# FoX values made token by token for four heads at once, the residual kept in DRAM during the heads, and gate tiles ahead of the scores

## The reference

```python
def fox_shared_kv(h, kv_norm_g, w_kv, b_forget):
    proj = rmsnorm(h, kv_norm_g) @ w_kv              # (528, 2048 + 2048 + 16)
    k, v, f_logit = jnp.split(proj, [D_INNER, 2 * D_INNER], axis=-1)
    ...                                              # 16 heads of 128 columns
    cum = jnp.cumsum(log_sigmoid(f_logit + b_forget), axis=1)

def fox_layer(h, norm_g, w_in, w_out, k, v, cum):
    q, r = jnp.split(rmsnorm(h, norm_g) @ w_in, 2, axis=-1)
    q = q.reshape(...) * FOX_HEAD_DIM ** -0.5
    for start, end in zip(bounds[:-1], bounds[1:]):  # causal blocks of 128 queries
        s = q[start:end] @ k[:end].T + cum[start:end, None] - cum[None, :end]
        p = softmax(where(causal, s, NEG_INF))
        outs.append(p @ v[:end])
    return h + (o * silu(r)) @ w_out
h = rmsnorm(h, final_norm_g); return h[:, N_META:]
```

## Time and profile before

| | us |
|---|---|
| median of 3 runs | 1025.69 (1025.11 to 1025.74) |
| time of the profiled execution | 1027.1 |
| span in its profile | 1025.3 |
| PE busy | 1013.7 (99%) |
| PEld busy | 950.4 (93%) |
| DVE busy | 638.4 (62%) |
| ACT busy | 521.8 (51%) |
| granted PE clock, mean | 0.996 |

### The profile page before, as it was taken

The page is one execution under the profiler, slowest core; times in us unless marked ns, Lnnn a source line. Parts: engine busy times, 40 slices in busy tenths (PEclk is TensorE's granted clock), DMA queues, the critical chain, the costliest instruction groups (busy, mean ns, idle before and its releaser), DMA issues.

```text
span 1025.3 us, 18641 instructions
## 1 busy us (share of the span) xinstructions
PE 1013.7 (99%) x7655; PEld 950.4 (93%) x7655; DVE 638.4 (62%) x1100; ACT 521.8 (51%) x932; POOL 34.3 (3%) x69
## 2 busy tenths in 40 slices
PE   8999999999999999999999999999999999999997
PEld 7999999999999999998999999999999999988886
DVE  6875666577567784447665656655656566576433
ACT  6754644654474553336554545454545555564321
POOL 0000000000000000000101000000000000010000
PEclk9999999999999999999999999999999999999998
DMA  8221221221122122222444333332434332331312
GB/s 286 70 77 63 83 84 49 76 83 64 62 87 79 63 70 96 91 96 65 135 110 89 110 89 86 94 102 89 110 97 102 104 94 77 99 87 67 119 42 82
DMA packets 34838, 92.98 MB, mean 91 GB/s; under 512 B 3888, under 2 KB 12976, under 8 KB 34752
## 3 DMA queue, kind: packets, MB, share of 16 engines
q1 hardware_dynamic: 34320, 91.62, 29.3%
q10 hardware_dynamic: 432, 0.15, 0.1%
HBM read 89.43 MB, written 2.13 MB: 89 GB/s over the span
## 4 chain that ended last, share of the span: by engine, by line
PE 98%; DMA 1%; DVE 0%; ACT 0%; issue 0%; DVEq 0%; SPq 0%; ACTq 0%
PE psum L1385 81%; PE psum L1701 3%; PE psum L1510 2%; PE psum L1684 2%; PE psum L1438 1%; PE psum L1458 1%; PE psum L1672 1%; PE psum L1671 1%; PE psum L1673 1%; PE psum L1506 1%; PE psum L1479 1%; DMA hT<-xT 1%; PE psum L1689 1%; PE psum L1504 0%; PE psum L1436 0%; PE psum L1408 0%
## 5 line engine op out<-in xcount | busy, mean ns | idle before, releaser
L820 DVE TENSOR_TENSOR w_lo<-raw,w_hi 128x1024 fp32r<-128x1024 f32 x143 | 173.5, 1223 | 28.4 <-ACT w_hi L431 28.3
L431 ACT ACTIVATE w_hi<-raw 128x1024 fp32r<-128x1024 f32 x143 | 149.6, 1052 | 34.8 <-PE psum L1385 34.1
L1385 PE MATMUL psum<-xh,w_hi 128*128 128x264 f32 x768 | 159.1, 288 | 2.7 <-DVE xl L842 1.5
L1385 PE MATMUL psum<-xl,w_hi 128*128 128x264 f32 x768 | 155.9, 285 | 0.0
L1385 PE MATMUL psum<-xh,w_lo 128*128 128x264 f32 x768 | 155.3, 283 | 0.0
L1385 PEld LDWEIGHTS psum<-xh,w_hi 128*128 128x128 f32 x768 | 118.5, 189 | 4.2 <-issue 2.3
L1385 PEld LDWEIGHTS psum<-xl,w_hi 128*128 128x128 f32 x768 | 119.5, 188 | 0.0
L1385 PEld LDWEIGHTS psum<-xh,w_lo 128*128 128x128 f32 x768 | 119.1, 189 | 0.0
L1385 PE MATMUL psum<-zh,w_hi 128*128 128x264 f32 x512 | 106.0, 288 | 0.0
L1385 PE MATMUL psum<-y_lo,w_hi 128*128 128x264 f32 (+2 forms) x400 | 104.8, 314 | 0.0
L1385 PE MATMUL psum<-zl,w_hi 128*128 128x264 f32 x512 | 104.0, 285 | 0.0
(11 more groups left out here) (266 smaller groups left out, 1851.3 us busy)
## 6 DMA issues: line engine op xcount, KB each, us to landing
raw<-w_all SPq DMA_DIRECT2D x143, 512.0 KB, 3.3
sub<-sums SPq DMA_DIRECT2D x16, 264.0 KB, 7.1
sub<-sums SPq DMA_DIRECT2D x16, 200.0 KB, 6.5
sub<-sums SPq DMA_DIRECT2D x16, 136.0 KB, 4.7
hT<-xT SPq DMA_DIRECT2D x8, 264.0 KB, 6.7
outT<-hT SPq DMA_DIRECT2D x8, 256.0 KB, 2.5
sub<-sums SPq DMA_DIRECT2D x16, 72.0 KB, 3.5
raw<-w_all SPq DMA_DIRECT2D x2, 256.0 KB, 5.1
```

The costliest lines, as they stand in the source:

```text
L431: nc.scalar.activation(w_hi[:, n % HI_RING, :], raw[:, n % LO_RING, :], ACT.Copy).then_inc(hi_made, 1)
L820: nc.vector.tensor_tensor(w_lo[:, n % LO_RING, :], raw[:, n % LO_RING, :], w_hi[:, n % HI_RING, :].bitcast(F32), ALU.subtract).then_inc(lo ...
L1385: i = nc.tensor.matmul(o, w[a][:, k % KT, :], x[b][:, k, c0:c1], start=k == first and a == b == 0, stop=k == last and a == 1)
```

## The change

- **Values by token.** The value strips, their copy and the transposes go. For four heads at once (a group) the normed activations `zh`, `zl` are stationary, a block of 128 tokens at a time, and the weights of the four heads move, 512 columns (`fox_values`). Banks 4 to 7 take the four blocks. ACT and DVE write `fv_hi`, `fv_lo` from there for all four heads, in the order of blocks 3, 2, 0, 1. Each chunk now holds two contraction tiles by 512 columns, four chunks to a group.
- **End tokens.** Their values come from a product in plain f32 of its own (`end_values`, job m): `z_end`, 16 tokens, is stationary, and the raw weights move, in four column groups of the array. ACT and DVE add up the four partial sums. The splits of a group's first chunks on DVE wait for it, since `w_lo` is written over `raw`.
- **Order.** Group 0 stands before the first head; a group g stands after head 4g-1. Before the scores of a head stand the first two contraction tiles of its gate strip r, three after a group; in the kernel before none (one in the last head).
- **Residual.** `fv_hi` and `fv_lo` now lie where `hT` lies. The 512 tokens of `hT` are stored to DRAM during the first layer's output product and loaded back after the last head's attention.

```diff
 def fox_step(h):
-    jobs = [f"r{h}"] + more[:1] + more[1:] + [f"a{h}"] + ([f"x{h + 1}"] if more else [])
-    return jobs + ([f"v{h + 2}"] if h + 2 < FOX_HEADS else [])
+    group = (h + 1) // VH if more and (h + 1) % VH == 0 else None
+    return ([f"r{h}"] + more[:1] + ([] if group is None else [f"m{group}"]) + more[1:] + [f"a{h}"]
+            + ([] if group is None else [f"u{group}"]))
...
-        + ["k0", "LOWF", "q0", "v0", "x0", "v1"] + [j for h in range(FOX_HEADS) for j in fox_step(h)] + [f"w{d}" for d in range(KT)])
+        + ["k0", "LOWF", "m0", "q0", "u0"] + [j for h in range(FOX_HEADS) for j in fox_step(h)] + [f"w{d}" for d in range(KT)])
...
+    elif _job[0] == "u":
+        PLACE[_job] = 8
...
+            keep = {CHUNK[f"W{d + 1}b"] + LO_RING: d for d in range(1, KT - 1)}
+            keep.update({CHUNK["W1b"] + LO_RING: 0, CHUNK["k0"] + LO_RING: KT - 1})
...
+                if n in keep:
+                    d = keep[n]
+                    sp.wait_ge(h_made, d + 1)
+                    sp.dma_start(h_keep[:, d, :], hT[:, d, META:T]).then_inc(h_kept, 16)
+                if n == CHUNK["w1b"] + LO_RING:
+                    done(sp, f"a{FOX_HEADS - 1}")
+                    for d in range(KT):
+                        sp.dma_start(hT[:, d, META:T], h_keep[:, d, :]).then_inc(h_back[d], 16)
...
+            def fox_values_hi(g):
+                done(act, f"u{g}")
...
+                for b in U_ORDER:
+                    nc.scalar.activation(fv_hi[:, b, :], bank(4 + b), ACT.Copy, scale=rtok[:, b:b + 1]).then_inc(fvhi_made, 1)
...
+            def fox_values_lo(g):
+                for n, b in enumerate(U_ORDER):
+                    dve.wait_ge(fvhi_made, NBLK * g + n + 1)
+                    nc.vector.scalar_tensor_tensor(fv_lo[:, b, :], bank(4 + b), rtok[:, b:b + 1], fv_hi[:, b, :].bitcast(F32),
+                                                   op0=ALU.mult, op1=ALU.subtract).then_inc(fvlo_made, 1)
...
+            def end_values(g):
...
+                for k in range(KT):
+                    r = 32 * (k % 4)
+                    w = raw[:, CHUNK[f"u{g}{k // 2}"] % LO_RING, :].rearrange("p (k n) -> p k n", k=2)
+                    i = nc.tensor.matmul(bank(slot(job), 0, VH * P, r, r + META), z_end[:, k, :], w[:, k % 2, :], start=k < 4, stop=k >= 4)
+                i.then_inc(job_done, 1)
...
+            def fox_values(g):
+                if g:
+                    pe.wait_ge(alo_made, 4 * VH * g)
...
+                    for k in (2 * part, 2 * part + 1):
+                        for b in range(NBLK):
+                            if g and k == 0 and b == NBLK - 1:
+                                pe.wait_ge(fy_made, VH * g)
+                            for a, p in ((0, 0), (0, 1), (1, 0)):
+                                i = nc.tensor.matmul(bank(4 + b), xk[a][:, k, b * BLK:(b + 1) * BLK], w[p][:, k % 2, :], start=k == a == p == 0,
+                                                     stop=k == KT - 1 and a == 1)
...
                 for b in range(NBLK):
+                    if h % VH == 0:
+                        pe.wait_ge(fvlo_made, NBLK * (h // VH) + (1, 1, 2, 4)[b])
...
             for h in range(H):
-                if h + 1 < H:
-                    fox_scores(h)
-                    strip_late(f"r{h}", xq)
...
+                n = 3 if h % VH == 0 else 2
...
+                late_part(f"r{h}", range(0, n))
+                fox_scores(h)
+                late_part(f"r{h}", range(n, KT)).then_inc(job_done, 1)
...
+                last = h + 1 < H and (h + 1) % VH == 0
+                if last:
+                    end_values((h + 1) // VH)
...
-                if h + 1 < H:
-                    pe.wait_ge(fvt_made, h + 2)
-                    transposed(f"x{h + 1}", fvt)
-                if h + 2 < H:
-                    strip(f"v{h + 2}", xk)
+                if last:
+                    fox_values((h + 1) // VH)
```

More of the change, by code:

```diff
@@ L76 @@
 HS = SEQ // 2
+VH = 4
 WARM = 12
@@ L240, in program @@
         t_diag = sq[:, 0, 0:SEQ]
-        fsr, fvt = sq[:, 0, 0:SEQ], sq[:, 1, :]
+        fsr = sq[:, 0, 0:SEQ]
+        z_end = f_raw
         z_lo = y_lo[:, :, 0:SEQ]
@@ L256, in slot, with end_groups @@
             return PLACE[job]
+        def end_groups(g):
+            i = 8 if g < NBLK - 1 else 12
+            return [y[0:META, i + n, 0:VH * P] for n in range(4)]
         def joined(b):
             return psum[:, (b + 1) * BANK - BLK:(b + 1) * BANK + T - BLK]
+        h_keep = nc.dram_tensor("h_keep", (P, KT, SEQ), F32, kind="Internal").ap()
         sums = nc.dram_tensor("sums", (FOX_HEADS, T), F32, kind="Internal").ap()
@@ L349, in wait_chunk_used @@
             name = CHUNKS[n]
-            if name[0] not in "Ww":
+            if name[0] == "u":
+                g, part = int(name[1]), int(name[2])
+                if part < VH - 1:
+                    eng.wait_ge(u_used, (VH - 1) * g + part + 1)
+                else:
+                    eng.wait_ge(job_done, JOB[f"u{g}"] + 1)
+            elif name[0] not in "Ww":
                 eng.wait_ge(job_done, JOB[name] + 1)
@@ L751, in _ @@
             queries_hi(0)
-            fox_value(0)
-            ahead("v0")
-            ahead("v1")
+            end_groups_out(0)
+            ahead("u00")
+            ahead("u01")
+            end_values_hi(0)
+            ahead("u02")
+            ahead("u03")
             fox_values_hi(0)
-            fox_value(1)
             for h in range(H):
+                g = (h + 1) // VH if h + 1 < H and (h + 1) % VH == 0 else None
                 ahead(f"r{h}")
@@ L1244, in _ @@
             fox_key(0)
+            done(dve, "m0")
+            ahead(f"W{KT - 1}b")
             x = slot("LOWF")
@@ L1297, in _ @@
                     z_low(0, 4)
+                elif g is not None:
+                    done(dve, f"m{g}")
+                    ahead(f"r{h}")
+                    ahead(f"k{h + 1}")
                 elif h + 1 < H:
@@ new lines, in fox_values @@
+            def fox_values(g):
+                if g:
+                    pe.wait_ge(alo_made, 4 * VH * g)
+                else:
+                    pe.wait_ge(f_sum, 3)
+                for part in range(VH):
+                    n = CHUNK[f"u{g}{part}"]
+                    pe.wait_ge(lo_made, n + 1)
+                    w = [m.rearrange("p (k n) -> p k n", k=2) for m in (w_hi[:, n % HI_RING, :], w_lo[:, n % LO_RING, :])]
+                    if g == 0 and part == 2:
+                        sums_by_token()
+                    for k in (2 * part, 2 * part + 1):
+                        for b in range(NBLK):
+                            if g and k == 0 and b == NBLK - 1:
[3 more added lines that the diff above has]
+                                                     stop=k == KT - 1 and a == 1)
+                    if part < VH - 1:
+                        i.then_inc(u_used, 1)
+                i.then_inc(job_done, 1)
@@ L1653, in _ @@
+            fox_values(0)
             S_AT = [(7, 272), (7, 0), (6, 0), (4, 0)]
```

207 lines of the change are left out of this document (117 added, 90 removed).

## The result

| | before | changed |
|---|---|---|
| median of 6 runs, us | 1025.72 (1025.11 to 1026.23) | 1033.36 (1031.68 to 1035.62) |
| ratio to before | | 1.0074 (95%: 1.0064 to 1.0084) |
| span of the profiled execution, us | 1025.3 | 1033.8 |
| its own time, us | 1027.1 | 1035.6 |

The change made the kernel slower by 7.6 us, where I had forecast it faster by 4.8. Lines of the changed kernel are its own: L1473 is what L1385 was, L1822 and L1824 are attention (L1701, L1703), L1790 the scores (L1671), L1732 the end tokens' product, L1766 the values' blocks, L750 and L1239 their write-out by ACT and DVE, L397 SP's load of a chunk.

A forecast was written before the change was run, and what follows sets the result against it. PE bounds the kernel, so only its sum counts: -102.6 + 89.6 + 7.4 = -5.6 us, plus 0.8 of write-out wait, -4.8, from 1025.7 to 1020.9 us. Own range 1019.6 to 1022.6; 8 in 10, 1019.0 to 1025.5.

The forecast's parts named there:

- The residual: Tail: eight loads back, issued at attention 15's end, cost 0; with slowest landing and a start 3 us later, 1.4 us.
- write-out, 4 groups: After each group's blocks, PE waits 0.1 to 0.3 us for the fourth bank; taken as 0.2, 0.8 in all.
- chunk for the end tokens: Before the end tokens' product: last raw chunk lands after 5.3 us, needed after 7.3; covered by 2 us.
- two gate tiles behind attention, 12 passages: Between attention and the next scores: two tiles take 1.40 us, moved there from the gate strip, not added.
- blocks, one group in the prologue and three: `fox_values`: 96 matmuls at 0.2332 us, 22.39 us a group, 89.6 for four; upper bound 90.6.
- PE's sum: PE's whole work: -102.6 for value strips and transposes, +89.6 blocks, +7.4 end tokens' product, giving -5.6 us.
- rival 1: Head passages: the 0.7 us margin before the scores goes, costing 3.6, 1024.5 us; heads of 22.95 or more; chance 0.13.
- a period of four heads: Sign in the changed profile: 115.0 us from scores to scores, where it was 116.2.
- rival 4: Wide matmuls stream faster with activations stationary: pitch down 7%, -6.3 us more, 1014.6 us; chance 0.04.
- rival 3: End tokens' product not four at once: 6.9 us a group instead of 1.84, 1041.2 us; chance 0.07.
- the way to the next scores: From q's end to the scores: 3.41 us on PE, bank 7 ready after 2.7; margin 0.7, cost 0.
- rival 2: Group's end: write-out exposed, ACT and DVE one after the other, 1.8 us a group, 1027.1; half, 1024.0; chance 0.08.

The follow-up runs named there:

- e1: Changed kernel with the residual's eight loads two chunk loads earlier in SP's queue: 1025.85 us, ratio to before 0.9998.
- e6: e1 with the next head's forget-sum loads, in heads 3, 7 and 11, issued after the group's fourth chunk load: 1023.88 us, ratio to before 0.9983.
- e5: e1 with four gate tiles instead of three ahead of the scores after a group: 1023.59 us, ratio to before 0.9981.
- e7: e1 with both the edits of e5 and e6: 1022.11 us, ratio to before 0.9964.
- e8: e1 with no gate tiles ahead of the scores in any head: 1048.22 us, ratio to before 1.0219.
- e2: Changed kernel with 20 small matmuls of zeros on PE before its wait for strip w2's bank: 1030.91 us, ratio to before 1.0048.

## Why the prediction was wrong

**The residual: this step failed.** I wrote that the eight loads "are issued at the end of attention 15" and gave them cost 0. The wait written in front of them is for attention 15, but SP takes its queue in order, and the first of the two chunk loads ahead of them, w3b, waits until w0b has been used, which is the end of strip w0: 947.15, not 941.5. They were issued 6.5 us late, and the first landed in 5.8 (the 3.0 to 6.8 of the earlier trace rows held). DVE's sum and its issue, which the forecast left out, took 0.84 more, and PE had 8.37 us of work: 6.49 + 5.83 + 0.84 - 8.37 = 4.79 us of wait, where I had 0. The bound that I kept, 1.4 us, supposed a start 3 us later; it was twice that, and the bound left out that PE came back from this wait at a granted clock of 0.50, some 2.5 us more. I had followed the waits of PE, DVE and ACT, and in SP's queue only the instruction itself. With this step right, the change comes out at 1025.85 (e1), which is still 5 us over the forecast of 1020.9: the tail was 7.5 of the 12.5 us by which the forecast missed 1033.36, the heads 4.3, and 0.7 stay unassigned.

**The heads: four terms mis-sized, two of them put at nothing.** The 4.3 us between the forecast -4.8 and the trace's -0.5:

| term | forecast, us | trace, us | difference |
|---|---|---|---|
| write-out, 4 groups | 0.8 | 4 x 0.44 | 1.0 |
| chunk for the end tokens | 0 | 0.22 + 0.41 + 0.83 | 1.5 |
| two gate tiles behind attention, 12 passages | 12 x 1.40 | 12 x 1.50 | 1.2 |
| blocks, one group in the prologue and three | 4 x 22.39 | 22.79 + 3 x 22.50 | 0.7 |

They sum to 4.4, 0.1 more than there is to explain; the end tokens' product adds under 0.1. The 0.44 is 619.52 - 615.00 = 4.52 us, less three tiles (2.10) and the scores (1.98). The write-out itself was foreseen to 0.05 us: DVE ended 3.49 us after the blocks, against 3.45. What I took too low is what a late operand costs PE: the fourth score came 0.2 us late by the list of waits, and its first matmul then took 0.39 us instead of 0.12. The chunk landed in 7.3 to 7.9 us where I had taken 5.3 from the earlier trace rows; there 4.3 us lay between the sums' loads and the chunk's, here 2.9, since the scores stand later. e6 shows that the sums' loads were what delayed it; that it is the shorter distance fits, but was not varied by itself. e5 and e6 took away these two terms, 1.8 and 1.5 us, and gained a little more by their traces, 2.15 and 1.57 (by the medians 2.3 and 2.0, by the ratios 1.7 and 1.5).

The third and fourth are, as far as the rows show, one mistake: I subtracted the transposes and the value strip whole, 6.41 us. In the trace of before, the first long pair behind the transposes takes 0.33 us instead of 0.24 (566.04 to 566.37); this seam remains, and the query strip's 5.79 for 5.60 had shown it too. Corrected, PE's sum is -5.6 + 1.9 + 0.1 = -3.6 us, and e7, in which nothing waits, measures -3.6 (-3.9 between the same rows of its trace).

Of the signs that the forecast named, the heads between groups took 22.76 us, nearer to its 22.65 than to rival 1's 22.95, and a period of four heads 116.2 (618.53 to 734.75), as long as before, not 115.0. Its own range was also added up wrongly: -5.6 + 1.0 + 1.6 + 0.5 gives 1023.2 at the upper end, not 1022.6. The measured time lies outside either.

**What held.** The pitch of 0.2332 us with the activations stationary (22.50 for 96, rival 4 falls); the end tokens' product at 1.72 to 1.91 us, four at once (rival 3 falls, and so does the estimate of 2.24 us from the 3.07 times in the Trainium skill's TensorE: Matmul & The Clock Gate, Part 3, which the page measured on four groups of rows, not of columns); the way to the next scores, where PE never waited with two tiles (rival 1 falls), while e8 shows that the margin was real: without the 1.50 us of tiles PE waited 0.88, which leaves 0.6 of the 0.7; the write-out bank by bank (0.44 us a group exposed, not the 1.8 of rival 2, which falls); softmax, for which PE never waited; q0's start, 1.76 us behind the end of the forget gates' product. The tail was none of my rivals; I had named it only in the last sentence, as what would make the forecast wrong altogether.

The Trainium skill's TensorE: Matmul & The Clock Gate, Part 1, says that an idle stretch puts the array's clock back to 1.2 GHz and activity restores it; this case's trace agrees, with 0.50 granted after a wait of 4.8 us and 1.00 behind the same wait filled with matmuls of zeros (e2).

## What to carry to other kernels

When a transfer is put in a queue that runs in order, as SP's does here, its start is set by every wait ahead of it in that queue: read them out to the one that ends last, and put a transfer that something waits for ahead of prefetches that nobody needs yet. On an engine that bounds the kernel, count a wait as its length plus the restart (0.24 us in e8), and look at the granted clock behind it: 4.8 us of wait cost 2.5 more in it, the waits of 0.88 us in e8 nothing. What is subtracted for removed matmuls is their share of the stream, without the seams to their neighbours, which stay.

## What the runs showed of the hardware

- At the lower clock the 512-column matmuls came 0.427 us apart (955.27 to 959.11 in nine steps), which is 512 columns at 1.2 GHz to the nanosecond. At the full clock they came 0.233 apart with the activations moving and 0.234 with the weights moving (22.50 us for 96), not the 0.213 that 512 columns at 2.4 GHz would be. What the other 9% are no run shows.
- Four column groups at once gave 16 instructions of 512 columns of plain f32 in 1.72 to 1.91 us, where one alone would take 431 ns (an estimate, the 222 ns for 264 columns scaled by columns): 3.6 to 4.0 at once.
- 20 matmuls of zeros held the granted clock at 1.00 through 4.5 us, so zeros for operands were enough for it here.
